# Softmax division by pairs of heads, and the causal triangle cut by GpSimd, in a decoder layer on one core

## The reference

```python
def blocked_causal_attention(q, k, v, cum=None):     # per head, 528 keys
    ...
    logits = jnp.einsum('bhqd,bhkd->bhqk', qb, kb) * scale
    if cum is not None:
        logits = logits + cum[:, :, s0:s1, None] - cum[:, :, None, :s1]
    causal = jnp.arange(s0, s1)[:, None] >= jnp.arange(s1)[None, :]
    logits = jnp.where(causal[None, None], logits, -jnp.inf)
    probs = jax.nn.softmax(logits, axis=-1)
    outs.append(jnp.einsum('bhqk,bhkd->bhqd', probs, vb))

def mixer_block(h, ...):
    u = rmsnorm(h, g_attn); proj = u @ w_in
    o_fox = attention(8 heads x 64, forget-gate bias cum)            # group A
    q = rmsnorm(cq) @ w_uq; kv = rmsnorm(ckv) @ w_ukv                # low-rank latents
    o_mla = attention(8 heads, 64 + 32 rotary, values 64)            # group B
    mix = concat([rmsnorm(o_fox, g_fox_out), rmsnorm(o_mla, g_mla_out)])
    return h + mix @ w_o

def hier_moe_block(h, ...):   # top 1 of 4 groups, then top 2 of 8 SwiGLU experts of 256
    ...
    y = y + combine[:, e:e + 1] * (silu(u @ w1[e]) * (u @ w3[e]) @ w2[e])
```

## Time and profile before

| | us |
|---|---|
| median of 3 runs | 723.79 |
| the runs | 727.7, 723.79, 723.64 |
| the profiled execution | 727.11 |
| its span in the profile | 725.6 |
| PE busy in the span | 607.1 (84%) |
| DVE busy | 265.2 (37%) |
| ACT busy | 190.3 (26%) |
| POOL busy | 115.1 (16%) |

### The profile page before, as it was taken

The page is one execution under the profiler, slowest core; times in us unless marked ns, Lnnn a source line. Parts: engine busy times, 40 slices in busy tenths (PEclk is TensorE's granted clock), DMA queues, the critical chain, the costliest instruction groups (busy, mean ns, idle before and its releaser), DMA issues.

```text
span 725.6 us, 9161 instructions
## 1 busy us (share of the span) xinstructions
PE 607.1 (84%) x3447; PEld 386.3 (53%) x3447; DVE 265.2 (37%) x527; ACT 190.3 (26%) x345; POOL 115.1 (16%) x130
## 2 busy tenths in 40 slices
PE   3699999999996997999999859988788878787740
PEld 2598688885653554665455535544444444444420
DVE  4652324235876475686355521111011111111105
ACT  5532223333321542333144402211111111111110
POOL 8100002110021125811200011111011101111012
PEclk9999899999998998999999969999999999999985
DMA  8900000019200001004000359999999999999948
GB/s 249 374 5 1 1 0 1 1 74 328 87 1 0 1 1 58 1 1 173 1 29 30 147 202 374 382 389 396 397 401 397 403 400 395 394 391 393 402 137 308
DMA packets 39055, 140.17 MB, mean 193 GB/s; under 512 B 8480, under 2 KB 10576, under 8 KB 30576
## 3 DMA queue, kind: packets, MB, share of 16 engines
q1 hardware_dynamic: 29680, 122.83, 44.2%
q0 software_dynamic: 4224, 8.53, 3.8%
q10 hardware_dynamic: 5120, 8.39, 3.2%
HBM read 131.28 MB, written 12.65 MB: 198 GB/s over the span
## 4 chain that ended last, share of the span: by engine, by line
PE 60%; DMA 15%; SPq 9%; DVE 8%; issue 5%; ACT 2%; POOL 1%; ACTq 0%; POOLq 0%; DVEq 0%
PE ps L1612 16%; DMA w<-in_w 10%; PE ps L1889 10%; PE ps L1651 6%; PE ps L1745 6%; PE ps L1731 5%; SPq L588 3%; PE ps L1797 3%; PE ps L1916 3%; SPq L595 3%; DVE sums_r L1369 2%; SPq L589 2%; PE ps L1707 2%; DMA x<-in_x 1%; PE ps L1849 1%
## 5 line engine op out<-in xcount | busy, mean ns | idle before, releaser
L1889 PE MATMUL ps<-w,xt 128*64 128x256 f32 x1024 | 132.7, 417 | 44.9 <-issue 33.4
L1889 PEld LDWEIGHTS ps<-w,xt 128*64 128x64 f32 x1024 | 87.3, 151 | 101.6 <-issue 75.8
L1477 DVE TENSOR_TENSOR xt<-ps,g_ffn_c 128x512 f32<-128x512 f32 x32 | 22.1, 692 | 233.0 <-PE ps L1849 233.0
L765 POOL DMA_INDIRECT xg<-u_rows,idx x32 | 29.8, 932 | 286.1 <-PE ps L1849 216.8
L1369 DVE RECIPROCAL sums_r<-ps 64x512 f32<-64x512 f32 x16 | 53.7, 3355 | 26.8 <-PE ps L1745 26.8
L1916 PE MATMUL ps<-w,hT 128*64 128x512 f32 x256 | 61.8, 604 | 0.0
L1038 ACT ACTIVATE hsb<-ps 128x256 f32<-128x256 f32 x32 | 12.3, 383 | 167.7 <-PE ps L1889 167.7
L1731 PE MATMUL ps<-qT,kT 68*128 68x400 f32 (+9 forms) x160 | 47.9, 424 | 0.0
L1745 PE MATMUL ps<-probT,vals 128*128 128x512 f32 (+4 forms) x160 | 43.4, 416 | 3.5 <-DVE mixT L1370 3.4
L1651 PE MATMUL ps<-w_oa,mixT 128*128 128x512 f32 x96 | 44.5, 599 | 0.9 <-issue 0.8
L972 ACT ACTIVATE probT<-ps 128x416 f32<-128x416 f32 (+1 forms) x48 | 26.1, 544 | 68.8 <-PE ps L1734 68.7
(11 more groups left out here) (278 smaller groups left out, 893.0 us busy)
## 6 DMA issues: line engine op xcount, KB each, us to landing
w<-in_w SPq DMA_DIRECT2D x96, 1024.0 KB, 26.4
y_rows<-yh ACTq DMA_DIRECT2D x64, 128.0 KB
w_oa<-in_w_o SPq DMA_DIRECT2D x1, 3072.0 KB, 17.4
x<-in_x SPq DMA_DIRECT2D x4, 512.0 KB, 8.8
w_in_v<-in_w_in SPq DMA_DIRECT2D x1, 2048.0 KB, 11.2
w_in_k<-in_w_in SPq DMA_DIRECT2D x1, 2048.0 KB, 16.2
w_in_q<-in_w_in SPq DMA_DIRECT2D x1, 2048.0 KB, 20.1
u_rows<-u2n SPq DMA_DIRECT2D x4, 512.0 KB, 2.6
```

The source lines that it names most:

```text
L765: pool.indirect_dma_start(out=xg[e % 2][:, :, :].rearrange("p k n -> p (k n)"), out_offset=None, in_=u2_rows, in_offset=bass.IndirectOffse ...
L1889: ins = pe.matmul(ps[j * slots:(j + 1) * slots, 2 + b, 0:F], xt[b][:, k, :], w13[s][:, j, k, :], start=(k == 0), stop=(k == DK - 1))
```

## The change

- The division goes by pairs of heads. ScalarE copies sums and output of each head out of PSUM (`copy_output`, two instructions of 64x512) into `sums_s` and `mixT`; `apply` of the next head and the up-projection wait for these copies. VectorE, once for two heads, takes the reciprocal of 128x512 sums in SBUF and multiplies `mixT` by it. `o_done` now counts pairs.
- The five `causal_t` matmuls of `score` go. In their place GpSimd sets the triangle in `probT` to zero with five selections for each head (`mask_probs`: 112, 128 and 16, 128 and 128 columns wide), and `apply` waits for them (`masked`). The mask of `score_maxes` stays.
- GpSimd's order becomes: selections of a head, and after some heads a chunk of the sum of squares for an earlier pair; after the last head of each attention the last chunk, which waits for the last division. Of the scaling of `w_o`, six chunks move ahead of all `narrow_mla` (between the attentions), one each behind the selections of heads 9 and 10.
- `sums_s` lies in ring slot 0, so expert 0 is loaded only after the last division.

The diff, without lines that only follow from these (semaphore declarations and the counts of `masks_made`, which fall by one):

```diff
@@ -260,8 +260,8 @@
         probT = [place(f"probT{b}", [P, 3, 512], F32, r_p + 6144 * b) for b in range(2)]
-        sums_r = place("sums_r", [P, SEQ], F32, r_p + 12288)
-        assert r_p + 12288 + SEQ * 4 <= r_s + 2 * ST
+        sums_s = [place(f"sums_s{b}", [P, SEQ], F32, ring + narrow + SEQ * 4 * b) for b in range(2)]
+        assert r_p + 12288 <= r_s + 2 * ST and narrow + 2 * SEQ * 4 <= SLOT
         scrap = place("scrap", [P, D], F32, r_s)
@@ -562,7 +563,7 @@
-            sp.wait_ge(max_scored, 2 * GS)
+            sp.wait_ge(o_done, GS // 2)
             load_expert(0, 0)
@@ -704,29 +702,49 @@
-            def sum_squares(group):
-
-                c0 = group * DK // 2
-                for c in range(c0, c0 + DK // 2):
-                    pool.wait_ge(o_done, 2 * c + 2)
-                    if c == c0:
-                        if group == 1:
-                            pool.wait_ge(mix_rooted, 1)
-                        step(pool.tensor_tensor(sq_sum[:, :], mixT[:, c, :], mixT[:, c, :], ALU.mult))
+            def mask_probs(ph):
+
+                for g in range(ph * H, ph * H + H):
+                    for b in range(3):
+                        pool.wait_ge(exped, 3 * g + b + 1)
+                        t = probT[g % 2][:, b, :]
+                        if b == 0:
+                            parts = [(t[:, 0:P - META], [[1, P - META]], META)]
+                        elif b == 1:
+                            parts = [(t[:, 0:P], [[1, P]], 0),
+                                     (t[:, L - P:L - P + META], [[1, META]], P - META)]
+                        else:
+                            parts = [(t[:, 0:P], [[1, P]], 0), (t[:, L - 2 * P:L - P], [[1, P]], 0)]
+                        for k, (part, pattern, base) in enumerate(parts):
+                            pool.affine_select(out=part, in_=part, compare_op=ALU.is_ge, fill=0.0, base=base,
+                                               pattern=pattern, channel_multiplier=-1
+                                               ).then_inc(masked if k == len(parts) - 1 else masked_half, 1)
+                    if g % H in (3, 5, 7):
+                        square_chunk(g // 2 - 1)
+                    if g in (H + 1, H + 2):
+                        scale_wo([WO_A + g - H - 1])
+                square_chunk((ph + 1) * DK // 2 - 1)
+
+            def square_chunk(c):
+
+                group, c0 = c // (DK // 2), c // (DK // 2) * DK // 2
+                pool.wait_ge(o_done, c + 1)
+                if c == c0:
+                    if group == 1:
+                        pool.wait_ge(mix_rooted, 1)
+                    step(pool.tensor_tensor(sq_sum[:, :], mixT[:, c, :], mixT[:, c, :], ALU.mult))
+                else:
+                    step(pool.tensor_tensor(sq_one[:, :], mixT[:, c, :], mixT[:, c, :], ALU.mult))
+                    ins = pool.tensor_tensor(sq_sum[:, :], sq_sum[:, :], sq_one[:, :], ALU.add)
+                    if c == c0 + DK // 2 - 1:
+                        ins.then_inc(sq_summed, 1)
                     else:
-                        step(pool.tensor_tensor(sq_one[:, :], mixT[:, c, :], mixT[:, c, :], ALU.mult))
-                        ins = pool.tensor_tensor(sq_sum[:, :], sq_sum[:, :], sq_one[:, :], ALU.add)
-                        if c == c0 + DK // 2 - 1:
-                            ins.then_inc(sq_summed, 1)
-                        else:
-                            step(ins)
-
-            def scale_wo():
-
-                pool.wait_ge(late_in, LATE * 16)
-                for c in range(DK):
-                    if c in (0, WO_A):
-                        pool.wait_ge(wo_in[c // WO_A], 16)
+                        step(ins)
+
+            def scale_wo(chunks):
+
+                for c in chunks:
+                    pool.wait_ge(wo_in[c // WO_A], 16)
                     pool.tensor_scalar(wo_chunk(c), wo_chunk(c), g_mix[:, c:c + 1], None, ALU.mult
@@ -741,11 +759,12 @@
                 narrow_fox(n, u)
-            sum_squares(0)
+            mask_probs(0)
+            pool.wait_ge(late_in, LATE * 16)
+            scale_wo(range(WO_A))
             for n, u in enumerate(up_units):
                 narrow_mla(n, u)
-            scale_wo()
-            sum_squares(1)
+            mask_probs(1)
@@ -971,12 +990,23 @@
+                def copy_output(g):
+
+                    to, by = out_rows(g), sum_rows(g)
+                    act.wait_ge(pv_done, g + 1)
+                    if g >= 4 and g % 2 == 0:
+
+                        act.wait_ge(o_done, g // 2 - 1)
+                    act.activation(sums_s[g // 2 % 2][to, :], ps[by, OUT, :], ACT.Copy).then_inc(o_copied, 1)
+                    act.activation(mixT[to, g // 2, :], ps[to, OUT, :], ACT.Copy).then_inc(o_copied, 1)
+
                 shift_row(g0)
                 for g in range(g0, g0 + H):
                     for b in range(3):
                         exp(g, b)
                     if g + 1 < g0 + H:
                         shift_row(g + 1)
+                    copy_output(g)
@@ -1363,11 +1393,12 @@
-                def normalise(g):
-                    to, by = out_rows(g), sum_rows(g)
-                    dve.wait_ge(pv_done, g + 1)
-                    step(dve.reciprocal(sums_r[to, :], ps[by, OUT, :]))
-                    dve.tensor_tensor(mixT[to, g // 2, :], ps[to, OUT, :], sums_r[to, :], ALU.mult
+                def normalise(m):
+
+                    dve.wait_ge(o_copied, 4 * (m + 1))
+                    dve.reciprocal(sums_s[m % 2][:, :], sums_s[m % 2][:, :]).then_inc(sums_inv, 1)
+                    dve.wait_ge(sums_inv, m + 1)
+                    dve.tensor_tensor(mixT[:, m, :], mixT[:, m, :], sums_s[m % 2][:, :], ALU.mult
                                       ).then_inc(o_done, 1)
@@ -1375,7 +1406,8 @@
                         row_maxes(g + 2)
-                    normalise(g)
+                    if g % 2:
+                        normalise(g // 2)
@@ -1636,7 +1668,7 @@
                 pe.wait_ge(wo_scaled, (group + 1) * DK // 2)
-                pe.wait_ge(o_done, (group + 1) * H)
+                pe.wait_ge(o_done, (group + 1) * H // 2)
                 if group:
@@ -1728,19 +1760,16 @@
                         wide = SEQ - q0
-                        pe.matmul(ps[:, b, c0:c0 + wide], kT[0:depth(g), h, block_cols(j)], qT[0:depth(g), h, q0:],
-                                  start=True, stop=False)
-                        m0 = META if j == 0 else P - META if j == MT else 0
-                        ins = pe.matmul(ps[:, b, c0:c0 + P - m0], identb[:, :], causal_t[:, m0:], start=False,
-                                        stop=True)
+                        ins = pe.matmul(ps[:, b, c0:c0 + wide], kT[0:depth(g), h, block_cols(j)],
+                                        qT[0:depth(g), h, q0:], start=True, stop=True)
                         if j in (0, MT, 3):
                             ins.then_inc(scored, 1)
                 def apply(g):
                     if g > g0:
-                        pe.wait_ge(o_done, g)
+                        pe.wait_ge(o_copied, 2 * g)
                     for n, (j, b, c0) in enumerate(KEY_BLOCKS):
-                        pe.wait_ge(exped, 3 * g + b + 1)
+                        pe.wait_ge(masked, 3 * g + b + 1)
                         q0 = first_query(j)
@@ -1768,12 +1797,13 @@
             pe.wait_ge(narrowed, sum(by_act(u) for u in turns))
-            pe.wait_ge(masks_made, 16)
+            pe.wait_ge(masks_made, 15)
             attend(0)
             pe.wait_ge(wup_in, 32)
-            pe.wait_ge(o_done, H)
+            pe.wait_ge(maxed, NT * H)
+            pe.wait_ge(o_copied, 2 * H)
```

More of the change, by code:

```diff
@@ L280, in build @@
         causal = new("causal", [P, P], BF16)
-        causal_t = new("causal_t", [P, P], BF16)
         last_rows = new("last_rows", [P, 1])
@@ L394, in build @@
         wo_in = [sem(f"wo_in{b}") for b in range(2)]
+        masked, masked_half = sem("masked"), sem("masked_half")
         rope_in, wo_scaled, fox_added = sem("rope_in"), sem("wo_scaled"), sem("fox_added")
```

8 lines of the change are left out of this document (3 added, 5 removed).

## The result

The changed kernel takes 712.64 us (median of 4, 711.57 to 715.01) where the kernel before, run beside it, takes 723.85: a ratio of 0.9835, 95% interval [0.9805, 0.9864]. It is faster by 1.65% by that ratio (the two medians are 1.55% apart); I had forecast 725.1 and no difference. The number is rival C's (712.8), though not quite its mechanism. The profiled execution took 711.57 (span 710.1) against 727.11 (725.6).

A forecast was written before the change was run, and what follows sets the result against it. VectorE closes each attention head's loop (6.89 us), TensorE hardly less full; the experts wait for weights. -5.4 + 8.5 - 4.4 + 1.25 = -0.05, or +2.85 with L1406 shut out; middle +1.3, so 725.1 us; range 712 to 732.

The forecast's parts named there:

- rival C: Between the attentions, GpSimd's scalings of w_o shut nothing out: staging at E + 11.5, total -11, 712.8 us; chance 0.13.
- E + 1.35: E is the first attention's end; the up-projection, waiting for two copies, was to start 1.35 us after it, before at 4.2.
- The clock falls: Between the attentions, TensorE waits over 12 us, then runs at 1.2 GHz: 2.4 us added (5 us at half rate).
- The load of expert 0: Its wait ends with the last division, some 20 us later; DMA engines nearly idle there, so counted as nothing.
- Rival E: In the heads, the new SBUF reciprocal shuts GpSimd's selections out, so `apply` waits: +7.8 on the sum, 732.9 us; chance 0.08.
- D: Between the attentions, scalings starve VectorE until E + 25.2; `turn_up(0)` at E + 29.2, 732.0 us; chance 0.08.
- L1387, L1388 and L1389 wait for one scaling each: Between the attentions, three VectorE prelude instructions each wait out a 2.84 us GpSimd scaling, ending at E + 17.0.
- the middle that I took: Between staging with L1406 free (`turn_up(0)` at E + 20.9) and shut out (E + 23.8); sums -0.05 and +2.85.
- the +1.3 of my sum: Whole kernel: predicted change against the profiled 727.11 us, giving 728.4, or 725.1 on the median; chance 0.60.
- by the longest wait that a row shows: Between the attentions, alternative bound: four waits of at most 1.07 cost 4.3, staging some 3 us earlier than before.
- the attentions: The two attention stretches were to shorten by 5.4 us (first) and 4.4 us (second).
- The masks: In each head, removing five mask matmuls from TensorE was to save 0.26 us, 0.05 for the first one.

The follow-up runs named there:

- the control: The changed kernel as it is, run again beside the kernel before in a later batch: 713.92 us, ratio 0.9838 to the kernel before.
- the probe: The changed kernel plus 36 small two-input products and 24 tensor-scalar instructions on VectorE while GpSimd's six scalings run: 722.07 us, one execution.

## Why the prediction was wrong

**What was right.** The first order of things: VectorE closes the loop, and only with it out of the way do the masks count (pairs alone 0.9936, selections alone 0.998, both 0.9835). The up-projection's start, E + 1.35, came at E + 1.39. The copies take 1.2, and no `apply` waits for `masked`. The last division ends 5.4 behind the last `apply`, and the product behind it is 1.25 later. The clock falls before the up-projection's third unit and costs 1.7, or 2.4 in the control (I had 2.4). The load of expert 0 costs nothing. Rival E fell, and D: VectorE was not starved.

**The step that failed** is "L1387, L1388 and L1389 wait for one scaling each: 8.1 + 3 x (2.84 + 0.1)", with L1419 behind them. I had one kind of row for two SBUF inputs beside GpSimd: a squares instruction, also of two inputs, that shut the rotation out for its whole 1.3 us. I carried "until it is done" over to an instruction of another form and twice the length. That one shuts such a product out in its first 1.0 us alone. So the four waits of 2.84 became none for L1387 and L1389, 0.7 for L1388 and 0.3 for L1419, and L1406 took 0.5 more: 1.5 in all. `turn_up(0)` was to be at E + 20.9 to 23.8 and was at 12.8: I had it 8 to 11 us too late, and by the middle that I took 9.5 of the 12.7 between the +1.3 of my sum and the -11.4 of the stages. The Trainium skill ("SBUF — State Buffer", section "Who interferes with whom") says that a VectorE instruction with two SBUF inputs contends with a GpSimd instruction that reads SBUF, and calls the shared ports an exclusive lock: whoever issues first has them for the whole instruction, and the other blocks fully. The squares here agree (1.30 against 0.23); for the scalings the probe measured 1.0 of 2.84, and the measurement decides. I had also given the bound "by the longest wait that a row shows, 1.07, four waits cost 4.3". The "some 3 us earlier than before" that I drew from it is a slip: C's E + 11.5 and 4.3 make E + 15.8, 1.0 later than before; 3.3 earlier is C, with no waits at all. Still it was the better estimate, 3.0 off where mine was 8 to 11 off, because it is made of a wait that a row shows, where the other one multiplied a rule by a length that no wait had ever had. Rival C had the right time with a mechanism half right: the scalings do shut something out, 1.5's worth, and the clock cost more than its 1, which the longer gain in the attentions made up for. That it came within 0.2 us is luck.

**Sizes that were off.** The masks: 0.26 a head in the sum, 0.42 measured. I took the time from the start of a mask to the next matmul in one row of a pair. The same rows had a better measure, 0.32: `score` takes 2.88 there (309.95 to 312.83), and the ten matmuls of `apply`, of the same widths and without masks, 2.56. With 0.16 more a head, 1.3 for eight, the attentions gained 7.0 and 6.0 in place of 5.4 and 4.4. **What was missed:** the output product's clock behind the longer idle time, +1.5 in four of the five executions (the probe among them) that had 2.0 idle and no constant products. In the profiled pair it doesn't show (the last column differs by 0.3), for that column varies by 2; but the three rows of the table whose output product ran at half clock average 374.4 there, the seven others 373.5.

By the stages, the sum against the profiled execution was to be +1.3 and was -11.4: attentions -3.2 beyond the forecast, staging -9.5 against the middle that I took, clock -0.7, the small rest +0.7.

**The chances.** I gave 0.60 to a mechanism whose evidence was rows of other instructions (a squares instruction of 1.3, a memset of 0.2), and 0.13 to the case that it does not carry over, of which I had written that only the lack of a row spoke for it. A lack of rows spoke against both alike. The range's lower end, 712, was C's, and held the time by 0.6.

## What to carry to other kernels

Where two edits each free a different engine of one loop, price them together: alone they gave 0.6% and nothing, together 1.65%. A stall seen beside one instruction need not last as long as the instruction that it meets elsewhere: here it was 1.07 of 1.3 beside the one, and at most 0.9 of 2.84 beside the other. Until a row shows more, the bound made of waits that were seen deserves at least as much weight as the rule. And where one engine's work makes TensorE's wait longer, count the lower clock that may come behind the wait too, or fill it with constant products.

## What the runs showed of the hardware

- A GpSimd multiplication by a column (128x1024 f32, 2.84 us) shuts out a VectorE product of two SBUF inputs in its first 1.03 us alone, and the tensor-scalar form there and in its last 0.9 to 1.0, with 0.8 free between (three scalings of one execution; the stretched rows of the changed kernel fit). A VectorE product that starts 0.03 or 0.04 behind the scaling still passes. A GpSimd product of two tensors (128x512, 1.3 us) shuts the former out for its whole length.
- A VectorE reciprocal from SBUF to SBUF (128x512, 3.35 us) and GpSimd's selections (0.27 each on average) don't touch one another, nor does the reciprocal's length depend on whether it reads PSUM or SBUF, 64 or 128 partitions (3.35 and 3.36).
- A bf16 mask matmul (16 to 128 columns, five a head) among f32 matmuls costs 0.084 us on average, while from its start to the next matmul is 0.05.
- The granted clock fell to its lower level (0.50 of full, 1.2 GHz) behind or within idle stretches of TensorE of 10.8 us (once), of 4.3 (four of four executions in which it was full before), of 3.8 (once), of 2.0 (four of five) and of 1.7 (twice), but not behind 2.8 in the one execution that had it, nor behind 1.6 and 1.3: the length of the last stretch alone doesn't decide.
